# Indices of a gather staged by pairs, consumers two boundaries behind TensorE, and gates on two bank pairs in turn

## The chip, the cores and the metric

The kernel runs on one core of one Trainium2 chip. The metric is the device time of one execution in microseconds; three executions of the kernel before took 2054.03, 2059.32 and 2064.04 us, median 2059.32.

## The reference

One step of a one-layer decoder for a prompt of 512 tokens and a sample group of 64 tokens (8 sequences of 8). Both run through the same layer, in float32:

```python
[q | k | v | u] = x @ w_in + b_in
att  = three dilated causal windows with ALiBi, merged by their softmax denominators
y    = S5 state-space groups over u; z = gelu(y); ssm = z * sigmoid(z @ w_glu + b_glu)
h    = LN1(ALPHA * x + concat(rms(att), rms(ssm)) @ w_out + b_out)
out  = LN2(ALPHA * h + PEER(h) + sigmoid(h @ w_ple_gate) * (p @ w_ple))

def PEER(x):                       # in blocks of 128 tokens, 8 heads
    q = x @ w_pq                   # two halves of 128 per head
    s1, s2 = q1 @ sub_keys1.T, q2 @ sub_keys2.T
    # top 16 of each, top 16 of their 256 sums -> 16 experts e of 16384, weights g = softmax
    a = gelu(x . peer_u[e]); return sum over 8 x 16 experts of g * a * peer_v[e]
```

The sample group attends to a cache of 2048 positions per sequence. Each token reads 128 rows of `peer_u` and 128 of `peer_v`, 1024 floats each; the kernel keeps both in one table, so a gathered row is 8 KB.

## The kernel before

Tokens are five blocks: four of 128 prompt tokens (b = 0 to 3) and one of 64 sample tokens (b = 4). A front part projects the input, runs the state-space scan and takes block 0 to its first experts. Then comes one long loop over the experts.

**The loop.** A step gathers one expert row for each of 128 partitions (1 MB) into one of eight ring slots (`RING`, `HALF` = 4, `PAIR` = 2). There are 576 steps, 288 pairs. A partition holds one (token, head part) item: four groups of 32 tokens share a block. For each pair, in program order on each engine:
- POOL (L803 to L812) waits until the indices are staged and the slot is free, and issues the gather.
- DVE (L2013) waits for the landing and multiplies the `u` half with `hrep`, h spread to the gather's layout, and sums: `dotted`.
- ACT (L1544 to L1560) waits for `dotted`; at the second pair of a half it copies the half's next four indices as integers (`copy_stage`, L1502, `staged`); then gelu, times the weight, and a 128x32 selection matrix for each slot (L1559, `diagonal`).
- PE (L1262) multiplies that matrix with the slot's `v` half, adds into two PSUM banks, and frees the slot (`slot_free`).

**The background.** All other work is put between pairs: attention of blocks 1 to 3 (`scores` L868 on PE, `bias` L1703 on DVE, `exps` L1349 on ACT, `turn_probs` L883 on PE, `copy_pt` L1358 on ACT, `values` L893 on PE, `norm_out` L1366 on ACT), output projections (`project` L1042, `residual_half` L1975), the questions to the key tables (`ask` L1208, `ask_out` L1484, `match` L1223, `match_out` L1492), the selection on DVE (`tops`, `cross`, `resolve`, L1887 to L1943) and `lay` (L1515) on ACT, decode attention on the cache (`s_scores` L1050, `s_values` L1096), and the gates (`gate` L1180, `gate_out` L1471 on ACT and L2024 on DVE, `finish`). `order_of_work` (L199) is a table written by hand: `at[p]` lists what stands at boundary p, ahead of pair p. Every engine walks through the same list in order and does its part of each entry; between engines there are only semaphores. So when ACT and PE both have a part at boundary p, ACT's part waits for PE's, and ACT's next pair behind it waits too.

**Block edges.** Blocks change at pairs 64, 128, 192 and 256. There h of the next block is spread: eight matmuls (`spread`, L1240) and eight copies into `hrep` (L1533), two of each at boundaries -3, -2, -1 and 0 of the edge. Around the edge the two slots of a pair belong to one group of 32 tokens (`token_groups`, L68).

**SP** (from L589) issues all other loads in a fixed order behind semaphores: weights as their places come free, the cache's keys and values for the eight sequences (`keys`, `values`, L672 to L681), then the sample block's and the gates' weights.

Of the kernel before, what the change touches and what calls it, by code (L numbers as in the profile page):

```python
# [17 lines left out]
P = 128  # L18
# [103 lines left out]
def order_of_front():  # L122
# [7 lines left out]
    for n in range(steps + 1):  # L130
# [38 lines left out]
        if n == 14:  # L169
# [5 lines left out]
              ("ask_out", 0, 1), ("ask_out", 0, 2), ("match", 0, 1)] + [("spread", 0, n) for n in range(8)]  # L175
# [9 lines left out]
ATT_AT = 2  # L185
GLU_AT = 7
RMS_AT = 33
PROJECT_AT = 33
LOOK_AT = 48
DECODE_AT = 128  # L190
DECODE_PAIRS = 8
SAMPLE_AT = DECODE_AT + DECODE_PAIRS * (NB - 1) + 10
SAMPLE_PICK_AT = SAMPLE_AT + 18
GATE_AT = SAMPLE_PICK_AT + 28
# [4 lines left out]
def order_of_work():  # L199
# [9 lines left out]
    at[GLU_AT + 2 * (QB - 1)].append(("take_sums",))  # L209
    for k in range((QB - 1) * NH // 2):  # L210
        two = [NH + 2 * k, NH + 2 * k + 1]
        qb = two[0] // NH
        t = ATT_AT + 2 * k
        for p, what in ((0, "scores"), (1, "bias"), (2, "exps"), (2, "turn_probs"), (3, "copy_pt"), (3, "invert"),
                        (4, "values"), (5, "norm_out")):
            at[t + p] += [(what, i) for i in two]
        if two[1] % NH == NH - 1:
            at[t + 6] += [("squares", qb), ("turn_att", qb)]
            at[t + 7].append(("att_out", qb))
            at[t + 8].append(("keep_squares", qb))  # L220

    def pick(n, *when):
# [3 lines left out]
        for x in range(2):  # L226
            at[when[4 + x]].append(("cross", b, c, x))
            at[when[6 + x]].append(("resolve", b, c, x))
            at[when[7] + 1 + x].append(("lay", b, c, x))

    def look(t, n):
# [3 lines left out]
        at[t + 2] += [("ask_out", b, c)]  # L235
        at[t + 3] += [("match", b, c)]
        at[t + 4] += [("match_out", b, c)]

    pick(1, *range(8))
    pick(2, *range(10, 26, 2))  # L240
    pick(3, *range(26, 42, 2))

    at[RMS_AT] += [("rms", 1), ("rms_root", 1)]
    at[RMS_AT + 1].append(("rms_inverse", 1))
    for b in range(1, QB):
        for half in range(2):
            t = PROJECT_AT + 4 * (b - 1) + 2 * half
            at[t].append(("project", b, half, 0))
            at[t + 1].append(("project", b, half, 1))
            at[t + 2].append(("residual_half", b, half))  # L250
        at[t + 3].append(("root", b))
        at[t + 4].append(("normal", b, 0))
        at[t + 5].append(("normal", b, 1))
    at[LOOK_AT - 7].append(("turn", 1))
    at[LOOK_AT - 6].append(("turn_out", 1))
    look(LOOK_AT - 5, 4)
    look(LOOK_AT, 5)
    for n in range(4, 4 * QB):
        t = LOOK_AT + 8 * (n - 4)
        pick(n, *range(t, t + 8))  # L260
        if n + 2 < 4 * QB:
            look(t + 2, n + 2)
        if n + 3 < 4 * QB and picks[n + 3][1] == 0:
            at[t + 7].append(("turn", picks[n + 3][0]))
            at[t + 8].append(("turn_out", picks[n + 3][0]))
# [12 lines left out]
    at[t].append(("s_gelu",))  # L278
    at[t + 1].append(("s_glu",))
    at[t + 2].append(("s_gate",))  # L280
    at[t + 3].append(("s_product",))
    at[t + 4].append(("s_att",))
    at[t + 5].append(("s_sums",))
    at[t + 6] += [("s_project", 0), ("s_scale",)]
    at[t + 7] += [("s_project", 1), ("rms_root", 2)]
    at[t + 8].append(("s_residual",))
    at[t + 9].append(("root", QB))
    at[t + 10].append(("normal", QB, 0))
    at[t + 11].append(("normal", QB, 1))
    at[t + 12].append(("turn", QB))  # L290
    at[t + 13].append(("turn_out", QB))
    look(t + 14, 4 * QB)
    for c in range(4):
        t = SAMPLE_PICK_AT + 8 * c
        pick(4 * QB + c, *range(t, t + 8))
        if c < 3:
            look(t + 2, 4 * QB + c + 1)

    for k, b in enumerate(FINISHED):
        t = GATE_AT + GATE_PAIRS * k  # L300
        at[t].append(("gate_turn", b))
        at[t + 1].append(("gate_turn_out", b))
        at[t + 2].append(("gate", b, 0, 0))
# [1896 lines left out]
```

## Time and profile before

| what | value |
|---|---|
| median of three runs | 2059.32 us |
| the profiled execution's own time | 2070.46 us |
| its span | 2068.6 us |
| mean granted TensorE clock | 0.856 |
| busy: PE, DVE, ACT, POOL | 1567.7, 1342.2, 776.8, 762.9 us |
| bytes moved | 718.95 MB, mean 348 GB/s |
| first gather issued | 293.9 us |
| last dot product starts | 2052.2 us |

Engines are PE (TensorE matmuls), PEld (its weight loads), DVE (VectorE), ACT (ScalarE), POOL (GpSimd) and SP (its queue issues plain DMAs). Times in the rows are microseconds from the span's start unless marked ns. "L1262" is a line of the kernel before. The clock is the share of full speed that was granted. A DMA share of 1.01 is full.

### The profile page before, as it was taken

How to read it: one execution, taken by the hardware profiler on the slowest of the kernel's cores; microseconds unless marked ns; L12 is line 12 of the kernel's file. 1: busy time of each engine (PE TensorE's matmuls, PEld its weight loads, DVE VectorE, ACT ScalarE, POOL GpSimd, SP SyncE). 2: the span in 40 equal slices, each digit the busy share in tenths (PEclk: the TensorE clock that was granted, in tenths of full speed). 3: DMA queues.
4: the chain of work that ended last, by engine and by line, in shares of the span. 5: the costliest groups of instructions: out<-in, count | busy, mean ns of one | idle time of the engine just before them, and what ended most of it. 6: DMA issues, size and time to landing. Idle time of an engine off the chain costs nothing.

```text
span 2068.6 us, 23469 instructions
## 1 busy us (share of the span) xinstructions
PE 1567.7 (76%) x7166; PEld 724.3 (35%) x7166; DVE 1342.2 (65%) x3188; ACT 776.8 (38%) x2630; POOL 762.9 (37%) x797
## 2 busy tenths in 40 slices
PE   7998696775877887767787766666885567789884
PEld 5674473332334343334322222222222234222221
DVE  6975647665768778888868444444344777655554
ACT  2132134764344444444444433323322333434442
POOL 0942213333334344444433333333233333443442
PEclk9999698788999989888898788878887886888987
DMA  7013157889999899999999999999999999988996
GB/s 282 1 62 102 70 205 325 332 325 398 396 384 420 349 380 421 419 419 415 413 393 412 401 421 410 422 413 424 359 412 423 422 421 381 402 333 334 364 358 279
DMA packets 103326, 718.95 MB, mean 348 GB/s; under 512 B 11696, under 2 KB 16560, under 8 KB 23600
## 3 DMA queue, kind: packets, MB, share of 16 engines
q0 software_dynamic: 82944, 604.02, 72.2%
q1 hardware_dynamic: 20272, 113.58, 13.8%
q8 instruction: 56, 0.92, 0.2%
q14 instruction: 54, 0.44, 0.1%
HBM read 712.69 MB, written 4.87 MB: 347 GB/s over the span
## 4 chain that ended last, share of the span: by engine, by line
PE 47%; DMA 26%; DVE 14%; ACT 6%; issue 6%; POOL 2%; POOLq 0%; ACTq 0%; SPq 0%; DVEq 0%
DMA R<-d_uv,W 25%; PE bank L1262 17%; DVE R L2013 8%; PE bank L854 5%; PE bank L1208 4%; PE bank L1050 3%; PE bank L1180 3%; PE bank L847 2%; POOL R L809 2%; ACT W L1554 2%; PE bank L1240 2%; PE bank L925 1%; PE bank L1096 1%; ACT W L1559 1%; ACT L1551 1%
## 5 line engine op out<-in xcount | busy, mean ns | idle before, releaser
L1262 PE MATMUL bank<-R,W 128*32 128x512 f32 x2304 | 794.2, 743 | 451.0 <-ACT W L1559 450.3
L809 POOL DMA_INDIRECT R<-d_uv,W x576 | 659.3, 1145 | 1114.6 <-ACT W L1502 536.3
L2013 DVE CUSTOM_DVE_ANT_0 R<-R,W 128x1024 f32<-128x1024 f32 x576 | 692.6, 1222 | 388.6 <-DMA R<-d_uv,W 385.2
L1262 PEld LDWEIGHTS bank<-R,W 128*32 128x32 f32 x2304 | 214.3, 125 | 928.2 <-ACT W L1559 637.5
L1502 ACT CAST W<-W 128x4 uint32<-128x4 f32 (+1 forms) x146 | 28.0, 193 | 453.8 <-DVE W L2013 453.6
L1559 ACT ACTIVATE W<-W 128x32 f32<-128x32 f32 x576 | 153.6, 314 | 9.4
L1551 ACT ACTIVATE W<-W 128x2 f32<-128x2 f32 x288 | 57.9, 201 | 254.2 <-DVE W L2013 253.2
L1554 ACT ACTIVATE W<-W 128x1 f32<-128x1 f32 x576 | 138.2, 287 | 10.3
L1551 ACT ACT_TABLE_LOAD x58 | 74.4, 1283 | 99.1 <-DVE W L2013 98.6
L854 PE MATMUL bank<-E,W 128*128 128x288 f32 x384 | 102.1, 424 | 11.7 <-DMA E<-d_xT 9.6
L1208 PEld LDWEIGHTS bank<-E 128*128 128x128 f32 x768 | 96.3, 207 | 26.4 <-issue 26.4
L1208 PE MATMUL bank<-E 128*128 128x128 f32 (+1 forms) x768 | 100.5, 294 | 0.0
L854 PEld LDWEIGHTS bank<-E,W 128*128 128x128 f32 x384 | 74.6, 198 | 33.3 <-issue 11.8
L1050 PE MATMUL bank<-E,W 128*64 128x512 f32 (+1 forms) x192 | 73.9, 527 | 0.0
L1180 PE MATMUL bank<-E 128*128 128x512 f32 (+1 forms) x160 | 73.1, 599 | 0.0
L1515 ACT COPY W<-E 32x16 f32<-32x16 f32 (+2 forms) x288 | 60.8, 211 | 7.3 <-DVE E L1943 3.9
L2024 DVE TENSOR_TENSOR W<-E,bank 128x512 f32<-128x512 f32 (+1 forms) x10 | 6.9, 687 | 76.3 <-ACT E L1471 76.3
L1887 DVE MAX8 E<-W 128x8 f32<-128x128 f32 (+3 forms) x120 | 40.1, 334 | 23.3 <-ACT W L1492 21.9
L1533 ACT COPY W<-bank 128x512 f32<-128x512 f32 x36 | 21.1, 586 | 88.2 <-PE bank L1240 88.2
L925 PE MATMUL bank<-E,R 32*128 32x128 f32 x256 | 34.5, 338 | 19.5 <-DVE R L1737 17.8
L2013 DVE DVE_READ_ACCUMULATOR2_ANT W<- 128x1 f32 x576 | 47.1, 82 | 0.0
L1042 PE MATMUL bank<-E 128*128 128x512 f32 x96 | 44.9, 610 | 0.0
(318 smaller groups left out, 1814.7 us busy)
## 6 DMA issues: line engine op xcount, KB each, us to landing
E<-d_kc SPq DMA_DIRECT2D x8, 2560.0 KB, 21.1
E<-d_w_pq SPq DMA_DIRECT2D x6, 2048.0 KB, 12.6
E<-d_vc SPq DMA_DIRECT2D x8, 1536.0 KB, 26.7
R<-d_uv,W POOLq DMA_INDIRECT x576, 10.9
E<-d_w_out SPq DMA_DIRECT2D x4, 2048.0 KB, 12.0
E<-d_vc SPq DMA_DIRECT2D x8, 1024.0 KB, 30.8
W<-d_w_in SPq DMA_DIRECT2D x3, 2048.0 KB, 18.1
R<-d_w_pq SPq DMA_DIRECT2D x3, 2048.0 KB, 13.0
```

The lines of the kernel that those rows point to most:

```text
L809: pool.indirect_dma_start(ring[r], None, A["uv"], bass.IndirectOffsetOnAxis(ap=stage[:, half, s:s + 1], axis=0),).then_inc(landed[r], 16)
L854: last = mm(bank[:, piece_bank(n), 0:WIDE], w[:, k, c * P:c * P + P], xT[:, k, x * WIDE:x * WIDE + WIDE], start=(k == 0), stop=(k == DC - 1))
L925: last = mm(bank[:, 6 + x, j * P:j * P + P], Bt[r, q, x, :], uT[r, q, b * P:b * P + P], start=True, stop=True)
L1050: last = mm(bankf[0:ST, n0:n1], qblk[:, b, c, :], kcS[:, c, n0:n1], start=(c == 0), stop=(c == CT - 1))
L1180: last = mm(bank[0:m, to, :], hT[:, k, 0:m], w[:, k, :], start=(k == 0), stop=(k == DC - 1), skip_group_check=True)
L1208: last = mm(bank[:, (2, 0)[c % 2], j * P:j * P + m], w[:, k, j * P:j * P + P], hT[:, k, 0:m], start=(k == 0), stop=(k == DC - 1))
L1262: last = mm(acc[TG * js[s]:TG * js[s] + TG, half * 512:half * 512 + 512], wsel[:, r, :], ring[r][:, D + half * 512:D + half * 512 + 512], ...
L1515: last = nc.scalar.copy(egall[TG * s:TG * s + TG, :, c0:c0 + (g1 - g0 - 1) * groups + 1:groups], eg[TG * j:TG * j + TG, :, 8 * s + g0 - 8 ...
L1551: f(gel[:, x, two], dots[:, x, two], ACT.Gelu_apprx_tanh).then_inc(gelued, 1)
L1554: last = f(wts[:, x, s:s + 1], gel[:, x, s:s + 1], ACT.Copy, scale=egall[:, 1, column(i, x * HALF + s, 1)])
L1559: f(wsel[:, x * HALF + s, :], fold[:, 0:TG], ACT.Copy, scale=wts[:, x, s:s + 1]).then_inc(diagonal, 1)
L2013: last = nc.vector.tensor_tensor_reduce(ring[r][:, 0:D], ring[r][:, 0:D], hrep[:, js[s], :], 1.0, 0.0, ALU.mult, ALU.add, dots[:, x, s:s + 1])
```

## The change

**Indices by pairs.** Both staging copies, ahead of the loop and in it, now cover two indices, one copy for every pair; POOL waits for `staged` ahead of each pair of gathers instead of each half.

**The table.** Consumers of PE's background work are put further behind it. `spread` is split: the copies are an entry of their own, `spread_out`, one boundary after the matmuls. In attention the bias stands two boundaries behind the scores (it was one), exponentials and transposes at +3, the copies at +5, the values at +6 and `norm_out` at +8 (they were at +2, +3, +4 and +5); steps still begin every two boundaries. `ask_out` stands two boundaries behind the last `ask`, `match_out` two behind `match`, the residual two behind the projection. The projections reach over 17 boundaries instead of 12. Block 1's first selection is squeezed into boundaries 54 to 59. Decode takes seven boundaries a sequence instead of eight and begins at 134 instead of 128.

**Gates.** `gate_out` on ACT becomes `gate_sigmoid`, two boundaries behind the matmuls, and the product on DVE one further; the two halves of a gate and the transposes of the next one use banks (0, 1) and (2, 3) in turn (`gate_banks`) instead of fixed ones. `finish`'s root is an entry of its own.

```diff
+    order += [(what, 0, n) for n in range(8) for what in ("spread", "spread_out")]
-        for p, what in ((0, "scores"), (1, "bias"), (2, "exps"), (2, "turn_probs"), (3, "copy_pt"), (3, "invert"),
-                        (4, "values"), (5, "norm_out")):
+        for p, what in ((0, "scores"), (2, "bias"), (3, "exps"), (3, "turn_probs"), (5, "copy_pt"), (5, "invert"),
+                        (6, "values"), (8, "norm_out")):
...
     for b in range(1, BLOCKS):
         for n in range(8 if b < QB else 4):
             at[BLOCK_PAIRS * b - 3 + n // 2].append(("spread", b, n))
+            at[BLOCK_PAIRS * b - 2 + n // 2].append(("spread_out", b, n))
...
+        def gate_banks(b, half):
+            return 2 * ((FINISHED.index(b) + half + 1) % 2)
...
             with pool.Fori(0, STEPS // RING) as i:
                 for half in range(2):
-                    pool.wait_ge(staged, 2 * i + half + 1)
                     for s in range(HALF):
                         r = half * HALF + s
+                        if s % PAIR == 0:
+                            pool.wait_ge(staged, i * (RING // PAIR) + (2 * half + s // PAIR + 1))
...
-                    pe.wait_ge(gate_used, 2 * n)
-                turn_h(b, BLOCKS + n)
+                    pe.wait_ge(gate_used, 2 * n - 1)
+                turn_h(b, BLOCKS + n, gate_banks(b, 1))
...
-                to = 2 - 2 * half
+                to = gate_banks(b, half)
                 if part == 0:
-                    pe.wait_ge(ht_ready, BLOCKS + FINISHED.index(b) + 1)
+                    pe.wait_ge(ht_ready, BLOCKS + n + 1)
+                    if half == 0 and n >= 1:
+                        pe.wait_ge(gate_used, 2 * n)
...
-            def copy_stage(half, at):
-                return nc.scalar.copy(stage[:, half, :], egall[:, 0, at])
+            def copy_stage(half, x, at):
+                return nc.scalar.copy(stage[:, half, PAIR * x:PAIR * x + PAIR], egall[:, 0, at])
...
-                h1 = p1 // 2
-                if (h1 + 1) * HALF < QB * EXP:
-                    act.wait_ge(laid, (h1 + 1) * HALF // (2 * PK) + 1)
+                last = (p1 + 2 * HALF // PAIR) * PAIR - 1
+                if last < QB * EXP:
+                    act.wait_ge(laid, last // (2 * PK) + 1)
...
                     act.wait_ge(dotted, n)
-                    if g == 1:
-                        copy_stage(x, column(i, RING + x * HALF, HALF)).then_inc(staged, 1)
+                    copy_stage(x, g, column(i, RING + x * HALF + g * PAIR, PAIR)).then_inc(staged, 1)
...
             def invert(i):
                 dve.wait_ge(p_ready, i + 1)
+                if i >= 4:
+                    dve.wait_ge(o_normed, i - 3)
...
-                tt(gp[0:m, n % 2, half * 512:half * 512 + 512], sgm[0:m], bank[0:m, 3 - 2 * half, :],
+                tt(gp[0:m, n % 2, half * 512:half * 512 + 512], sgm[0:m], bank[0:m, gate_banks(b, half) + 1, :],
```

POOL's loop, the first half of the ring, before:

```order
L807 ISA [waits staged]
L809 DMA R<-d_uv,W 128x2048 [waits slot_free]
L807 REGISTER_ALU
L809 DMA R<-d_uv,W 128x2048 [waits slot_free]
L807 REGISTER_ALU
L809 DMA R<-d_uv,W 128x2048 [waits slot_free]
L807 REGISTER_ALU
L809 DMA R<-d_uv,W 128x2048 [waits slot_free]
L803 REGISTER_ALU
L807 REGISTER_ALU [waits staged]
```

and after:

```order
L830 ISA [waits staged]
L832 DMA R<-d_uv,W 128x2048 [waits slot_free]
L830 REGISTER_ALU
L832 DMA R<-d_uv,W 128x2048 [waits slot_free]
L828 REGISTER_ALU
L830 REGISTER_ALU [waits staged]
L832 DMA R<-d_uv,W 128x2048 [waits slot_free]
L830 REGISTER_ALU
L832 DMA R<-d_uv,W 128x2048 [waits slot_free]
```

The wait for `staged` stood ahead of four gathers and now stands ahead of two.

ACT at the edge to block 1 before, from the weights of the fourth pair ahead of the edge on (L1533 are the copies of the spread, L1502 stages the indices, L1551 to L1559 are one pair):

```order
L1559 ACTIVATE W<-W 128x32 [waits weighed]
L1559 ACTIVATE W<-W 128x32
L1533 COPY W<-bank 128x512 [waits spread_full] x2
L1502 CAST W<-W 128x4 [waits dotted,laid]
L1551 ACTIVATE W<-W 128x2
L1554 ACTIVATE W<-W 128x1 [waits gelued]
L1554 ACTIVATE W<-W 128x1
L1559 ACTIVATE W<-W 128x32 [waits weighed]
L1559 ACTIVATE W<-W 128x32
```

and after, where the copies are L1562, the staging L1531 and a pair L1578 to L1586:

```order
L1562 COPY W<-bank 128x512 [waits spread_full] x2
L1531 CAST W<-W 128x2 [waits dotted,laid]
L1578 ACTIVATE W<-W 128x2
L1581 ACTIVATE W<-W 128x1 [waits gelued]
L1581 ACTIVATE W<-W 128x1
L1586 ACTIVATE W<-W 128x32 [waits weighed]
L1586 ACTIVATE W<-W 128x32
L1562 COPY W<-bank 128x512 [waits spread_full] x2
L1531 CAST W<-W 128x2 [waits dotted,laid]
```

The rows look alike; what moved is that the same two copies now stand behind one pair more of ACT's than of PE's matmuls, and each pair has its own cast.

PE in the attention steps before, one step with two pairs of experts (L893 values, L883 transposes, L868 scores, L1262 experts):

```order
L893 MATMUL bank<-E 128x64 [waits o_normed,pt_ready]
L893 MATMUL bank<-E 128x64
L893 MATMUL bank<-E 128x64 [waits o_normed,pt_ready]
L893 MATMUL bank<-E 128x64
L883 MATMUL bank<-ident,E 128x128 [waits pt_ready,p_ready]
L883 MATMUL bank<-ident,E 128x128 x2
L883 MATMUL bank<-ident,E 128x128 [waits pt_ready,p_ready]
L883 MATMUL bank<-ident,E 128x128 x2
L868 MATMUL bank<-E 128x384 [waits sc_biased] x2
L1262 MATMUL bank<-R,W 32x512 [waits diagonal]
L1262 MATMUL bank<-R,W 32x512
L1262 MATMUL bank<-R,W 32x512 [waits diagonal]
```

and after (L906 transposes, L1288 experts, L916 values, L891 scores):

```order
L906 MATMUL bank<-ident,E 128x128 [waits pt_ready,p_ready]
L906 MATMUL bank<-ident,E 128x128 x2
L906 MATMUL bank<-ident,E 128x128 [waits pt_ready,p_ready]
L906 MATMUL bank<-ident,E 128x128 x2
L1288 MATMUL bank<-R,W 32x512 [waits diagonal]
L1288 MATMUL bank<-R,W 32x512
L1288 MATMUL bank<-R,W 32x512 [waits diagonal]
L1288 MATMUL bank<-R,W 32x512
L916 MATMUL bank<-E 128x64 [waits o_normed,pt_ready]
L916 MATMUL bank<-E 128x64
L916 MATMUL bank<-E 128x64 [waits o_normed,pt_ready]
L916 MATMUL bank<-E 128x64
```

Values, transposes and scores stood together; now the transposes stand at one boundary and the values with the scores at the next, with a pair of experts between.

## Rows read from the trace of the kernel before

**Rows 1.** Busy PE, PEld, DVE, ACT, POOL by stretch, us; clock, DMA share, GB/s.
```profile
320.00:2052.00 1732.00, 1282.01 (x5324) 531.46 (x5324) 1117.78 (x2687) 692.57 (x2399) 652.68 (x570) 0.85 0.97 393
345.00:500.00 155.00, 110.81 (x488) 54.84 (x488) 107.29 (x305) 100.09 (x304) 54.20 (x52) 0.82 0.90 343
500.00:600.00 100.00, 80.18 (x246) 31.09 (x247) 66.62 (x134) 35.37 (x130) 32.27 (x28) 0.89 0.96 389
700.00:750.00 50.00, 41.81 (x160) 17.60 (x161) 35.46 (x97) 23.66 (x78) 15.66 (x17) 0.93 0.80 309
750.00:1000.00 250.00, 182.05 (x837) 88.82 (x835) 218.40 (x596) 111.41 (x456) 109.99 (x98) 0.85 1.01 419
1000.00:1050.00 50.00, 39.10 (x148) 16.91 (x145) 36.46 (x97) 22.60 (x87) 20.09 (x17) 0.90 1.01 390
1050.00:1460.00 410.00, 283.91 (x1467) 103.59 (x1466) 209.40 (x465) 142.94 (x494) 140.40 (x126) 0.82 1.01 415
1460.00:1500.00 40.00, 34.38 (x157) 10.57 (x156) 14.80 (x24) 12.82 (x48) 10.03 (x9) 0.82 0.87 341
1700.00:1750.00 50.00, 39.08 (x144) 21.18 (x142) 37.49 (x101) 15.17 (x57) 18.27 (x16) 0.70 0.95 378
1800.00:1850.00 50.00, 42.88 (x126) 16.40 (x124) 30.25 (x51) 23.42 (x64) 25.46 (x18) 0.90 0.93 363
1850.00:1890.00 40.00, 35.20 (x78) 9.51 (x77) 17.80 (x29) 13.95 (x38) 12.04 (x11) 0.83 0.70 264
1890.00:2050.00 160.00, 127.71 (x362) 42.19 (x364) 83.77 (x139) 63.36 (x186) 70.94 (x54) 0.87 0.94 376
```

**Rows 2.** DMA queues of the page: packets, MB, share.
```profile
q0 software_dynamic: 82944, 604.02, 72.2%
```

**Rows 3.** Waits, whole span: us in total, times, longest.
```profile
POOL R L809 <- ACT W L1502: 536.3, 87, 27.3
POOL R L809 <- PE bank L1262: 456.8, 175, 8.4
...
ACT W L1533 <- PE bank L1240: 88.2, 36, 9.2
...
DVE W L2024 <- ACT E L1471: 76.3, 10, 14.2
```

**Rows 4.** Timeline, 419 to 425 us: start, length, idle before and releaser.
```profile
419.81 1.92 PE L1262 MATMUL bank<-R,W 128*32 128x512 f32 x8
419.91 0.56 DVE L1703 CUSTOM_DVE_ANT_0 E<-bank,E 128x384 f32<-128x384 f32 x1 [6.38 <-PE bank L868]
...
424.84 0.94 POOL L809 DMA_INDIRECT R<-d_uv,W  x1 [7.67 <-ACT W L1502]
```

**Rows 5.** The page's costliest groups: the cast that stages indices.
```profile
L1502 ACT CAST W<-W 128x4 uint32<-128x4 f32 (+1 forms) x146 | 28.0, 193 | 453.8 <-DVE W L2013 453.6
```

**Rows 6.** Timeline at two block edges.
```profile
710.57 0.59 ACT L1533 COPY W<-bank 128x512 f32<-128x512 f32 x1 [7.03 <-PE bank L1240]
...
712.99 0.94 POOL L809 DMA_INDIRECT R<-d_uv,W  x1 [12.69 <-ACT W L1502]
...
1861.05 6.50 PE L1262 MATMUL bank<-R,W 128*32 128x512 f32 x8 [1.74 <-ACT W L1559]
...
1863.15 0.69 DVE L2024 TENSOR_TENSOR W<-E,bank 128x512 f32<-128x512 f32 x1 [14.19 <-ACT E L1471]
```

**Rows 7.** Waits, 350 to 500 us.
```profile
DVE E L1703 <- PE bank L868: 25.6, 9, 6.4
```

**Rows 8.** DMA issues of the page: count, KB each, us to landing.
```profile
E<-d_kc SPq DMA_DIRECT2D x8, 2560.0 KB, 21.1
...
E<-d_vc SPq DMA_DIRECT2D x8, 1024.0 KB, 30.8
```

**Rows 9.** Busy time of L1358 alone by stretch.
```profile
345.00:500.00 155.00, 9.89 (x22) 0.82 0.90 343
```

**Rows 10.** Busy time of L1366 alone by stretch.
```profile
345.00:500.00 155.00, 6.11 (x24) 0.82 0.90 343
```

More of the change, by code:

```diff
@@ L184 @@
 BLOCK_PAIRS = EXP // PAIR
-ATT_AT = 2
+ATT_AT = 1
 GLU_AT = 7
[L187 to L194, printed above, removed]
+PROJECT_AT = 35
+LOOK_AT = 54
+DECODE_AT = 134
+DECODE_PAIRS = 7
+SAMPLE_AT = DECODE_AT + DECODE_PAIRS * (NB - 1) + 13
+SAMPLE_PICK_AT = SAMPLE_AT + 20
+GATE_AT = SAMPLE_PICK_AT + 24
 GATE_PAIRS = 8
@@ L234, in look, with project, norm @@
         at[t + 1] += [("ask", b, c, 1)]
[L235 to L256, printed above, removed]
+        at[t + 3] += [("ask_out", b, c)]
+        at[t + 4] += [("match", b, c)]
+        at[t + 6] += [("match_out", b, c)]
+    pick(1, *range(10))
+    pick(2, *range(10, 26, 2), 25, 26)
+    pick(3, *range(26, 42, 2), 41, 42)
+    t = PROJECT_AT
+    at[t + 1].append(("rms", 1))
+    at[t + 2].append(("rms_root", 1))
+    at[t + 3].append(("rms_inverse", 1))
+    def project(b, half, t, u):
+        at[t].append(("project", b, half, 0))
+        at[t + 1].append(("project", b, half, 1))
+        at[u].append(("residual_half", b, half))
+    def norm(b, t):
+        at[t].append(("root", b))
+        at[t + 1].append(("normal", b, 0))
+        at[t + 2].append(("normal", b, 1))
+    project(1, 0, t, t + 3)
+    project(1, 1, t + 2, t + 5)
+    norm(1, t + 6)
+    project(2, 0, t + 4, t + 7)
+    project(2, 1, t + 6, t + 9)
+    at[t + 9].append(("turn", 1))
+    norm(2, t + 11)
+    at[t + 11].append(("turn_out", 1))
+    project(3, 0, t + 10, t + 13)
+    look(t + 12, 4)
+    project(3, 1, t + 14, t + 17)
+    norm(3, t + 24)
     look(LOOK_AT, 5)
@@ L323, in order_of_work @@
             order += at[p]
-    return order + [("finish", QB, 0), ("finish", QB, 1)]
+    return order + [("finish", QB, 0), ("finish_root", QB), ("finish", QB, 1)]
 ORDER = order_of_work()
@@ L1156, in turn_h @@
                 for c in range(DC):
-                    last = nc.tensor.transpose(bank[:, c // 4, (c % 4) * P:(c % 4) * P + m],
+                    last = nc.tensor.transpose(bank[:, first + c // 4, (c % 4) * P:(c % 4) * P + m],
                                                hB[b][0:m, c * P:c * P + P], ident[0:m, 0:m])
@@ L1470, in gate_out @@
                     act.wait_ge(gate_used, n)
-                f(sgm[0:m], bank[0:m, 2 - 2 * half, :], ACT.Sigmoid).then_inc(gate_sig, 1)
+                f(sgm[0:m], bank[0:m, gate_banks(b, half), :], ACT.Sigmoid).then_inc(gate_sig, 1)
             def turn_out(b):
```

109 lines of the change are left out of this document (59 added, 50 removed).

## The prediction

> **What bounds the kernel now.** I read the view by stretches first, then the waits of the whole span, then the timeline at the places where the transfers run thin. From 320 to 2052 us the core moves 393 GB/s with its DMA engines 97% busy, while PE, DVE and ACT are busy for 1282, 1118 and 693 of 1732 us [rows 1]. The work there is 576 gathers of 604.02 MB in all, 1.05 MB each [rows 2]. In the undisturbed stretch from 750 to 1000 us the rate is 419 GB/s at a full DMA share [rows 1], so a gather takes 2.5 us and a pair of them 5.0. The loop is bound by transfers wherever the ring of eight slots is kept supplied, and it loses time only where it is not. At 419 GB/s the 1732 us would be 1732 x 393/419 = 1625: at most 107 us can come back, whatever the edit. The 320 us before and the 16 us after the last gathers are a chain that the change hardly touches.
>
> The Trainium skill, DMA: Bandwidth & Descriptors, section Specifications, gives about 358 GB/s as HBM's limit for one core. By that rule no edit of the order could gain anything here; the trace disagrees, with 419 over 250 us, and the trace decides. The fabric ceiling of 435 GB/s in the same table is kept by every row; by it the most that can come back would be 167 us instead of 107.
>
> Where the 107 us lie, each as length x (1 - rate/419) [rows 1]:
> - 345 to 500, attention of blocks 1 to 3 in the background: 28.1 us. 500 to 600, projections: 7.2.
> - The four block edges, at 700 to 750: 13.1; 1000 to 1050: 3.5; 1460 to 1500: 7.4; 1850 to 1890: 14.8. Together 38.8 us.
> - Gates, 1800 to 1850: 6.7; 1890 to 2050: 16.4. Together 23.1 us.
> - The sample block's projection and questions, 1700 to 1750: 4.9. Decode, 1050 to 1460: 3.9.
>
> Together 106.0 us.
>
> **Staging by pairs.** POOL waited 536.3 us for the staged indices (ACT L1502) and 456.8 us for PE to free a slot [rows 3]. Where transfers are full this costs nothing. Where they aren't it does: PE's eight matmuls of a pair end at 419.81 + 1.92 = 421.7 us, which frees two slots, but POOL, idle for 7.67 us, issues only at 424.84, released by the cast that stages four indices at once after the next pair's dot products [rows 4]. With pairs the first two indices would be there before the slots, and two of four gathers go out about 424.84 - 421.7 = 3 us earlier. That is 3 us more slack in every half ring, before the transfers run dry. In return ACT casts twice as often: 144 casts more at 193 ns [rows 5], 28 us. ACT is busy for 693 of 1732 us [rows 1], so it lies beside DVE's dots. It stands ahead of the gelu, so where the ring is thin it delays the weights: some 470 us of such stretches hold about 90 pairs, half of them with a new cast, 45 x 0.19 = 9 us at most, zero at best. I take 2, since the wait behind it ends in most rows on a landing or on DVE.
>
> **Block edges.** Today the copy of the spread h (ACT L1533) stands at the same boundary as its matmul (L1240). PE reaches that only after the previous pair's matmuls, and ACT can't weigh the next pair meanwhile: it waits 7.03 us until 710.57, POOL 12.69 until 712.99 [rows 6]. ACT's waits there sum to 88.2 us [rows 3]. After the change ACT weighs one pair between, so the copy finds a finished matmul. What comes instead: PE's third and later spreads wait for copies that stand behind that pair's weights on ACT, and the first pair of a block waits for all eight copies, two of them behind its own weights. PE needs those weights anyway; what is added is two copies of 0.59 us [rows 6]. What stays is that the edge pairs of matmuls take 6.5 us at 1861 [rows 6], more than the 5.0 of a pair's transfers. Bounds: nothing or all of 38.8. I take two thirds, 26 us: ACT's wait is what made POOL's gap, and what stays is the small excess of slow matmuls.
>
> **Attention.** In 350 to 500 us DVE stood for 25.6 us for scores (L1703 behind L868) [rows 7], 6.38 of them at 419.91 [rows 4]; they are queued on PE behind the values and behind the transposes, which wait for the exponentials. The change puts transposes and scores at different boundaries and the bias two boundaries behind. But DVE is busy for 107 of 155 us in 345 to 500, ACT for 100 and PE for 111 [rows 1]; in 155 - 28 = 127 us that would be 84, 79 and 87%, with every engine in order. So the bounds are 0 and 28, and I take half, 14 us. For the projections there is little engine wait to remove: 3 of 7.2.
>
> **Gates.** DVE waited 76.3 us for sigmoids in ten places [rows 3], 14.19 of them until 1863.15, where it held the dot products back [rows 6]. Afterwards the sigmoid stands two boundaries behind PE, the product one behind it, and the next turn goes to the other bank pair. PE is busy for 43 of 50 us from 1800 to 1850 and for 128 of 160 from 1890 to 2050 [rows 1], though, so it is the next to bind. Bounds 0 and 23; half, 11 us. The sample block: 2 of 4.9, since the granted clock was 0.70 there [rows 1] and its matmuls stay long.
>
> **Decode** is packed from eight to seven pairs. The bytes are the same, so this moves load, it removes none: 0. Keys are issued when the previous scores end; six boundaries become five, 5 x 5.0 = 25 us at least, against 21.1 us from issue to landing [rows 8]. The values, 30.8 us [rows 8], keep six boundaries: 30 us at the bare rate of gathers, more with the cache's own bytes among them. Bounds: 0 and 8 x 0.8 = 6 us of late values.
>
> **Sum.** 26 + 14 + 3 + 11 + 2 - 2 = 54 us. The profiled execution took 2070.46 us for a span of 2068.6; 2070.5 - 54 = 2016.5. The median of the runs shown is 2059.3, 0.5% below the profiled one, so the forecast is 2059.3 x 2016.5/2070.5 = 2005.6, say 2006 us. Its own range, with a third to three quarters of the 107 coming back, is 1982 to 2024.
>
> **Rivals.**
> - Nearly everything comes back: 80% of 107 is 86, 2059 - 85 = 1974. For it speaks that two separate slacks are added, 3 us in the staging and a boundary in the background; against it the engine loads at attention and the gates. 0.12.
> - Half as much comes back, 27 us: 2032. DVE and PE become the bound in the attention stretch, where they would have to be 84 and 87% busy in order, and PE at the gates; only the edges give what I take. 0.18.
> - No change, 2056: the slots aren't free earlier than the indices in most thin places (POOL's 456.8 us behind PE speak for it), and the edges lose the same time to slow matmuls. Against it are the gaps of rows 6, all of which end on ACT. 0.07.
> - Slower: where consumers stand further back, buffers come free later, and PE meets that at the very boundary at which it refills them. Per attention step of two pairs the next scores now wait for the previous biases, two of 0.56 us [rows 4], the next transposes for the previous copies, 9.89/22 x 2 = 0.9 us [rows 9], and the values for the previous normalisations, 6.11/24 x 2 = 0.5 us [rows 10]; each was a boundary earlier before. If PE stands through all of it, 12 steps cost 12 x 2.5 = 30 us and give none of their 14; at the edges PE then waits for ACT's copies as ACT waited for PE, and the 26 don't come. Left are 3 + 11 + 2 - 2 = 14 us of gain: 2059 + 30 - 14 = 2075. It decides from the point where PE gets to a boundary before ACT and DVE have left it, that is, where a pair's matmuls take less than its weights and background on ACT; today they take 1.92 us at 419.81 and 6.50 at 1861.05 [rows 4, 6], so at full clock it can, at half clock it can't. 0.11.
>
> **How the numbers follow.** The forecast has 0.52. A measurement of this kernel tells a change from about 0.5%, 10 us. Faster by more: 0.52 + 0.12 + 0.18 less 0.01 = 0.81; within 0.5%: 0.07 and that 0.01, 0.08; slower 0.11. The range reaches from 1974 to 2052: it holds the forecast, the half case and most of the large one, and leaves out most of the slower case.
>
> **What would show it.** Right: the rate from 700 to 750 us and at the later edges over 390 GB/s; ACT's waits for the spread under 30 us in all; DVE's waits for sigmoids under 25; DVE's wait for scores under 10; POOL's waits for ACT much shorter and those for PE longer; the stretch of 345 to 500 at 380 GB/s. Wrong: the rates in these stretches unchanged, with PE's waits for ACT and DVE at the attention steps grown by some 2 us each; or waits of PE's cache matmuls on their loads.

## The result and the profile after

| | before | changed |
|---|---|---|
| median of the comparison, us | 2061.68 (2054.03 to 2064.04) | 2026.99 (2023.65 to 2035.52, 4 runs) |
| ratio, 95% interval | | 0.9844 [0.9802, 0.9886] |
| median, measured a second time | 2063.74 | 2027.54 (2024.40 to 2031.51) |
| its ratio | | 0.9818 [0.9785, 0.9852] |
| profiled execution, us; span | 2070.46; 2068.6 | 2025.18; 2023.4 |

The change takes off 32 to 38 us; the forecast was 54, 2006 us against 2027. The time lies in the range (1974 to 2052) and just outside the forecast's own (1982 to 2024). "Faster by over 0.5%" came true. The profiled executions differ by 45 us, more than the medians: before's took 0.4% longer than the median of its comparison. The traces say where time went, the medians how much there was.

The view by stretches of the changed kernel, in the columns of [rows 1]:

```profile
320.00:2007.00 1687.00, 1248.89 (x5323) 516.99 (x5324) 1120.62 (x2687) 706.58 (x2538) 669.92 (x569) 0.87 0.99 403
345.00:500.00 155.00, 110.35 (x504) 51.99 (x502) 112.48 (x318) 104.43 (x329) 61.19 (x55) 0.85 0.96 388
500.00:600.00 100.00, 86.34 (x292) 34.06 (x289) 70.86 (x135) 40.41 (x152) 39.07 (x33) 0.90 1.00 406
650.00:720.00 70.00, 62.67 (x260) 30.26 (x260) 49.02 (x121) 32.25 (x118) 25.74 (x21) 0.93 0.81 302
750.00:1000.00 250.00, 180.76 (x911) 94.62 (x908) 222.16 (x607) 113.59 (x473) 114.70 (x100) 0.91 1.01 420
1000.00:1040.00 40.00, 34.36 (x124) 14.37 (x122) 33.90 (x90) 20.12 (x81) 13.89 (x12) 0.91 0.94 358
1450.00:1490.00 40.00, 36.03 (x182) 13.52 (x180) 15.88 (x34) 14.78 (x50) 11.98 (x12) 0.88 0.94 375
1830.00:1870.00 40.00, 40.00 (x101) 12.62 (x100) 22.34 (x36) 20.37 (x60) 18.16 (x14) 1.00 0.89 350
1870.00:2007.00 137.00, 107.85 (x332) 34.43 (x332) 78.44 (x126) 59.42 (x177) 53.60 (x48) 0.91 0.98 394
```

The whole loop now runs at 403 GB/s, from 393; the undisturbed stretch stays at 420. Attention went from 343 to 388 GB/s and the gates from 376 to 394. The first block edge stays thin, at 302 GB/s for 70 us, with PE busy for 62.7 of them, and none of the four edges reaches the 390 GB/s that the prediction asked for: 302, 358, 375 and 350 in the rows from 650, 1000, 1450 and 1830 us. The waits of the whole span (total, times, longest):

```profile
POOL R L832 <- PE bank L1288: 833.2, 263, 16.3
...
POOL R L832 <- ACT W L1531: 104.0, 16, 27.7
...
ACT W L1562 <- PE bank L1266: 62.7, 32, 7.4
...
DVE E L1732 <- PE bank L906: 10.7, 8, 3.4
DVE W L2055 <- ACT E L1497: 7.5, 2, 7.2
```

Against [rows 3]: DVE's wait for sigmoids fell from 76.3 to 7.5 us, and its wait for the scores (25.6 us in [rows 7]) is gone, while 10.7 us of waits for PE's transposes (L906) are new; ACT's wait for the spread fell only from 88.2 to 62.7, where under 30 was expected. POOL's wait for the casts fell by 432 us and its wait for PE grew by 376.

A rate over a fixed window mixes pairs that have moved. So the two timelines are also set against each other by the work itself: from the start of one pair's dot product to that of another, us. At 5.0 us for a pair's transfers the bound is in the last column.

```
pairs                                    before    after   change   at 5.0 us
0-32     attention in the background      204.9    184.8    -20.1       160
32-60    projections                      168.4    170.4     +2.0       140
60-76    first block edge                  94.2     97.7     +3.5        80
76-122                                    230.8    230.7     -0.2       230
122-140  second edge                      118.3    116.6     -1.7        90
140-186  decode of the sample group       304.1    310.4     +6.3       230
186-198  third edge                        90.5     82.4     -8.1        60
198-240                                   252.2    248.8     -3.4       210
240-252  gates                             71.3     63.1     -8.2        60
252-256  gates, fourth edge's spreads      27.0     19.1     -8.0        20
256-264  fourth edge, pairs behind it      54.3     48.4     -5.9        40
264-287                                   124.1    124.0     -0.1       115
start of the first pair                   309.5    308.4     -1.1
behind the start of the last pair          18.9     18.5     -0.4
```

The sum is the difference of the spans, 45.2, but for rounding. The sample block has half as many spreads as the others, and all four stand at boundaries 253 and 254 (`range(8 if b < QB else 4)` in the table), so the fourth edge begins in the row of 252 to 256, which it shares with the gates. Attention gave 20 us where 14 were forecast. The four edges, of which 26 us were expected, gave 20 with that row, but all of it at the third and fourth (22.0); the first two, worth 11 in the forecast, lost 1.8. The gates gave 8.2 up to pair 252 and a part of the 8.0 behind it, for 11. The decode's row grew by 6.3, where 0 was expected.

### The profile page after: what moved, and what is told of

Read it like the earlier page. It is cut to its first block, busy times and chain, and to the rows that moved or that the text cites. A ratio compares the mean times of both kernels' runs of the same rounds, so it can differ in the third digit from the quotient of the medians.

```text
span 2023.4 us, 23729 instructions
## 1 busy us (share of the span) xinstructions
PE 1535.5 (76%) x7166; PEld 709.8 (35%) x7166; DVE 1345.0 (66%) x3188; ACT 791.9 (39%) x2776; POOL 780.0 (39%) x797
## 4 chain that ended last, share of the span: by engine, by line
PE 43%; DMA 31%; DVE 13%; ACT 6%; issue 5%; POOL 1%; POOLq 0%; ACTq 0%; SPq 0%; DVEq 0%
DMA R<-d_uv,W 31%; PE bank L1288 15%; DVE R L2044 7%; PE bank L877 5%; PE bank L1206 3%; PE bank L1234 3%; PE bank L1073 3%; PE bank L870 2%; PE bank L1266 2%; PE bank L948 1%; ACT W L1581 1%; PE bank L1119 1%; POOL R L832 1%; PE bank L1202 1%; ACT L1578 1%
## 5 line engine op out<-in xcount | busy, mean ns | idle before, releaser
L1288 PE MATMUL bank<-R,W 128*32 128x512 f32 x2304 | 764.1, 720 | 433.9 <-ACT W L1586 433.3
L832 POOL DMA_INDIRECT R<-d_uv,W x576 | 677.4, 1176 | 1053.2 <-PE bank L1288 833.2
L1288 PEld LDWEIGHTS bank<-R,W 128*32 128x32 f32 x2304 | 208.8, 122 | 877.0 <-ACT W L1586 592.4
L1531 ACT CAST W<-W 128x2 uint32<-128x2 f32 x292 | 55.6, 191 | 870.1 <-DVE W L2044 869.9
L1586 ACT ACTIVATE W<-W 128x32 f32<-128x32 f32 x576 | 153.5, 313 | 9.4
L1234 PEld LDWEIGHTS bank<-E 128*128 128x128 f32 x768 | 87.6, 192 | 20.5 <-issue 20.5
L1234 PE MATMUL bank<-E 128*128 128x128 f32 (+1 forms) x768 | 91.5, 277 | 0.0
L877 PEld LDWEIGHTS bank<-E,W 128*128 128x128 f32 x384 | 74.6, 198 | 32.2 <-issue 10.7
L1578 ACT ACTIVATE W<-W 128x2 f32<-128x2 f32 x288 | 57.5, 200 | 0.9
L1918 DVE MAX8 E<-W 128x8 f32<-128x128 f32 (+3 forms) x120 | 40.0, 333 | 21.5 <-ACT W L1520 19.9
L1562 ACT COPY W<-bank 128x512 f32<-128x512 f32 x36 | 20.9, 587 | 62.7 <-PE bank L1266 62.7
L1921 DVE MAX8 E<-W 128x8 f32<-128x128 f32 (+3 forms) x120 | 40.5, 338 | 4.1
## 6 DMA issues: line engine op xcount, KB each, us to landing
E<-d_vc SPq DMA_DIRECT2D x8, 1536.0 KB, 25.5
```

Of the source, the lines that this page charges most:

```text
L832: pool.indirect_dma_start(ring[r], None, A["uv"], bass.IndirectOffsetOnAxis(ap=stage[:, half, s:s + 1], axis=0),).then_inc(landed[r], 16)
L877: last = mm(bank[:, piece_bank(n), 0:WIDE], w[:, k, c * P:c * P + P], xT[:, k, x * WIDE:x * WIDE + WIDE], start=(k == 0), stop=(k == DC - 1))
L1234: last = mm(bank[:, (2, 0)[c % 2], j * P:j * P + m], w[:, k, j * P:j * P + P], hT[:, k, 0:m], start=(k == 0), stop=(k == DC - 1))
L1288: last = mm(acc[TG * js[s]:TG * js[s] + TG, half * 512:half * 512 + 512], wsel[:, r, :], ring[r][:, D + half * 512:D + half * 512 + 512], ...
L1531: return nc.scalar.copy(stage[:, half, PAIR * x:PAIR * x + PAIR], egall[:, 0, at])
L1578: f(gel[:, x, two], dots[:, x, two], ACT.Gelu_apprx_tanh).then_inc(gelued, 1)
```

## The experiments

Each was measured in five rounds against the kernel before, whose median was 2063.7 us in the first group, 2066.2 in the second and 2065.1 in the third (the split alone, the step with scores apart and the last two kernels), which ran on another chip. The changed kernel itself ran in the first group only. Differences between experiments are differences of their ratios times 2062, and "the changed kernel" is then its second measurement (0.9818), taken in the same way; by the first (0.9844) every loss would be 5 us smaller and every gain 5 us larger. Each ratio is known to 5 to 7 us either way, so a difference of two of them under some 9 us isn't clear of the noise by the ratios alone; where a smaller one is used, the single times and the pair times of the traces are given with it.

### Is the result firm? The changed kernel again

> The changed kernel itself, as the yardstick for its neighbours on the same chip: ratio 0.984 to the kernel before, within 0.976 to 0.990.

2027.54 us, ratio 0.9818 [0.9785, 0.9852]. This is the level that the others of its kind are set against. Its ten executions in both measurements took 2023.65 to 2035.52 us. Between the traces of its two profiled executions the pair rows differ by up to 2.2 us.

### Staging by pairs alone, and the change without it

The first adds only the casts by pairs to the kernel before:

```diff
+                        if s % PAIR == 0:
+                            pool.wait_ge(staged, i * (RING // PAIR) + (2 * half + s // PAIR + 1))
...
-                    if g == 1:
-                        copy_stage(x, column(i, RING + x * HALF, HALF)).then_inc(staged, 1)
+                    copy_stage(x, g, column(i, RING + x * HALF + g * PAIR, PAIR)).then_inc(staged, 1)
```

> The kernel before with staging by pairs alone. Theory (staging gives 3 us of slack in each half ring, so it helps wherever ACT and DVE hold the ring, and POOL's wait moves from ACT to PE): 12 to 20 us faster, ratio 0.990 to 0.994, POOL's waits for ACT under 200 us. Rival (the gain is all in the order of the background; the slots are not free earlier than the indices): ratio 0.998 to 1.002, though POOL's waits change their name all the same.

2063.47 us, ratio 0.9995 [0.9973, 1.0017]: nothing that can be told, within 5 us either way. Its waits over the span, and from 350 to 500 us:

```profile
POOL R L810 <- PE bank L1263: 860.4, 246, 11.4
...
POOL R L810 <- ACT W L1504: 106.2, 15, 27.3
```

```profile
POOL R L810 <- PE bank L1263: 83.8, 22, 6.8
...
DVE E L1705 <- PE bank L869: 25.5, 7, 6.5
```

POOL's waits are much like those of the full change: 536 us behind the cast have become 106, and 457 behind PE 860. The time has not moved, and the stretch of 345 to 500 us runs at 345 GB/s, from 343. A wait can change its name almost completely and be worth nothing. Two reasons are possible, and no run tells them apart: the slots were the next release all along, or the gathers that went out earlier were not what DVE stood for. One pair row moved without moving the total: 122 to 140 took 124.8 us, from 118.3, so a few us in that row tell little. In the kernel before, DVE stood in 350 to 500 us for the scores for 25.6 us [rows 7] and for landings for less:

```profile
DVE R L2013 <- DMA R<-d_uv,W: 10.4, 5, 5.4
```

The second is the changed kernel with the casts by halves again:

> The changed kernel with the indices staged by halves again. If the two parts add up, 0.990 to 0.994 of staging is given back: ratio 0.990 to 0.995 to the kernel before. Rival (the background's order alone carries the gain): ratio 0.984, as the changed kernel. Third (the parts only work together, since with the background loosened the staging becomes the last wait): ratio 0.995 to 1.0.

2023.57 us, ratio 0.9808 [0.9775, 0.9841]: the same as with pairs. No gain of the staging shows in either company.

### The copy of the spread: back to its matmul's boundary, and the split alone

```diff
-            at[BLOCK_PAIRS * b - 2 + n // 2].append(("spread_out", b, n))
+            at[BLOCK_PAIRS * b - 3 + n // 2].append(("spread_out", b, n))
```

> The changed kernel with the copies of the spread back at the same boundary as its matmuls. Theory (PE bounds the edges, so it matters little who waits for whom): all four edges together 0 to 8 us slower than the changed kernel, ratio 0.982 to 0.986 to the kernel before. Rival (the added boundary is what gave the 14 us that the edges gained in the trace): 12 us or more slower, ratio 0.988 or above, with the last edge (pairs 256 to 264) back at 54 us from 48.

2057.53 us, ratio 0.9971 [0.9949, 0.9993]: 31 us of the gain are gone, and the rival of the expectation came true. In the trace the first edge's pairs take 105.5 us (from 97.7), the second's 128.8 (116.6), the third's 88.3 (82.4), pairs 252 to 256 25.5 (19.1) and 256 to 264 52.2 (48.4). ACT's wait for the spread is twice that of the changed kernel:

```profile
ACT W L1562 <- PE bank L1266: 123.3, 36, 14.1
```

The other way round, the kernel before with nothing but the split (the copy as an entry of its own, one boundary behind the matmul; the line that places it):

```diff
+            at[BLOCK_PAIRS * b - 2 + n // 2].append(("spread_out", b, n))
```

> The kernel before with the copies of the spread one boundary behind its matmuls, and nothing else. Theory (the split is worth some 30 us by itself; the changed kernel shows only half of it because its table puts questions on the first two edges): ratio 0.984 to 0.989, pairs 60 to 76 in 84 us or less, 122 to 134 in 74 or less. Rival (the split helps only together with the rest of the table): ratio 0.993 to 1.0.

2038.85 us, ratio 0.9888 [0.9859, 0.9917]: 23 us from this one edit. Here the first edge is cured as the prediction had it: ACT's wait for the spread falls from 88.2 [rows 3] to 10.5 us, and 650 to 720 us run at 409 GB/s.

```profile
ACT W L1535 <- PE bank L1242: 10.5, 18, 2.2
```

```profile
650.00:720.00 70.00, 60.42 (x235) 25.58 (x232) 61.72 (x169) 36.83 (x143) 31.05 (x27) 0.93 1.00 409
```

The same window holds earlier pairs here than in the changed kernel, whose pair 60 starts at 663.6 us and this one's at 680.2. Pairs 60 to 76 take 83.6 us at 402 GB/s, against 94.2 before and 97.7 in the changed kernel (359 and 337 GB/s). The expectation's other mark was missed: pairs 122 to 134, at the second edge, took 88.5 us where 74 or less was expected and the kernel before took 83.8 (88.8 with the staging alone), so no gain shows there. The third edge's row gave 6.0 us, pairs 252 to 256 gave 5.1 and 256 to 264 4.9. So the split works at the first edge, and something else in the change takes its gain back there.

### What takes it back: questions at the edge

PE's timeline in the changed kernel at the first edge (start, length, idle before and releaser; L1288 experts, L1234 questions, L1249 match, L1266 spread):

```profile
669.96 2.12 PE L1288 MATMUL bank<-R,W 128*32 128x512 f32 x8 [1.62 <-ACT W L1586]
...
686.70 3.62 PE L1288 MATMUL bank<-R,W 128*32 128x512 f32 x8
690.25 1.16 PE L1249 MATMUL bank<-E,W 128*128 128x128 f32 x8
691.24 3.74 PE L1234 MATMUL bank<-E 128*128 128x128 f32 x32
694.91 1.98 PE L1266 MATMUL bank<-E,W 32*128 32x512 f32 x4
696.82 3.62 PE L1288 MATMUL bank<-R,W 128*32 128x512 f32 x8
700.37 3.84 PE L1234 MATMUL bank<-E 128*128 128x128 f32 x32
704.14 1.98 PE L1266 MATMUL bank<-E,W 32*128 32x512 f32 x4
```

From there to 715 us PE has a single gap, of 0.68 us. Behind a pair of experts (3.6 us at an edge, against 2.1 at 669.96) stand questions (3.8) and two spreads (2.0), 9.3 us from 696.82 to 706.12 for a pair whose transfers take 5.0. ACT and POOL stand behind it:

```profile
705.29 0.59 ACT L1562 COPY W<-bank 128x512 f32<-128x512 f32 x1 [6.04 <-PE bank L1266]
```

```profile
711.42 1.45 POOL L832 DMA_INDIRECT R<-d_uv,W  x1 [9.23 <-PE bank L1288]
```

Over 679 to 716 us PE was busy for 36.32 of 37 us at the full clock, while the transfers ran at 270 GB/s:

```profile
679.00:716.00 37.00, 36.32 (x143) 16.02 (x143) 24.24 (x63) 14.50 (x48) 11.22 (x12) 1.00 0.75 270
```

The table of the background was shifted with the longer attention (`LOOK_AT`, where its look-ups start, is 54 instead of 48), and with that a block of questions for the next tokens, two batches of 3.8 us and a match, falls on boundaries 63 and 64, where the spreads are. One more block falls on 127 and 128, at the second edge. In the kernel before the questions stood at 58 and 59 and again from 66 on, and at 122 and 123. The first experiment moves the block of boundaries 63 to 69 four boundaries on:

```diff
-            look(t + (5 if starts or n == 4 else 1), n + 2)
+            look(t + (5 if starts or n in (4, 5) else 1), n + 2)
```

> The changed kernel with one question block (two asks of 3.8 us each and a match) moved from boundaries 63 to 68 to 67 to 73, off the first block edge. Theory (PE is the bound there, busy without a gap from 679 to 716 us): pairs 60 to 70 in 59 us instead of 66, the whole 5 to 8 us faster, ratio 0.978 to 0.980. Rival (DVE and ACT hold the ring there): the same 66 us and ratio 0.982.

2018.09 us, ratio 0.9777 [0.975, 0.9804], 8 us below the changed kernel, and all six executions (2011.78 to 2021.26) lie below its ten. Pairs 60 to 76 take 90.4 us instead of 97.7, and the edge runs at 349 GB/s:

```profile
650.00:720.00 70.00, 61.71 (x250) 29.17 (x251) 53.91 (x131) 34.55 (x124) 28.21 (x24) 0.93 0.90 349
```

That is half of the way to the 83.6 us of the split alone. The other suspect is the length of PE's expert pairs at the edges, where both slots of a pair go to the same 32 columns. Here they go to two groups, which changes what is summed there:

```diff
-                    js = token_groups(2 * i + x if isinstance(i, int) else p0 // 2)
+                    js = list(range(SG)) if m == P else [0, 1, 0, 1]
```

> The changed kernel, with PE's expert matmuls of the pairs at the block edges put into two groups of 32 columns as in the rest of a block, where the changed kernel has both slots of a pair in one group (this changes what is summed there; nothing else differs). Theory (PE bounds the edges: a pair takes 3.62 us at full clock there instead of 2.12): 4 edges x 4 to 8 pairs x 1.5 us, of which the starved ones count, 10 to 20 us faster than the changed kernel, ratio 0.975 to 0.979 to the kernel before, and over 370 GB/s from 650 to 720 us instead of 302. Rival (DVE and ACT hold the ring ahead of the first edge, with the squeezed selection, the normalisation and 5 us of lay): no change, 0.984, and the thin stretch from 655 to 720 stays.

2016.47 us, ratio 0.9773 [0.9735, 0.981]: 9 us below (2012.36 to 2025.26). Relieving PE at the edges in either way gives about the same; both say that PE's own work is a part of what binds there. ACT's wait for the spread goes to 44.5 us (from 62.7). It isn't all of it: the expectation asked for over 370 GB/s, and the row reaches 326, with PE busy for only 53.7 of the 70 us:

```profile
650.00:720.00 70.00, 53.71 (x266) 28.12 (x262) 52.82 (x127) 32.34 (x118) 28.69 (x26) 0.88 0.84 326
```

Block 1's squeezed selection on DVE (boundaries 54 to 59) and block 3's normalisation (59 to 61) stand ahead of this edge in the changed table too. No run moved them.

### Attention and gates at their old distances

The changed kernel with the old attention steps (one boundary between producer and consumer, scores with values and transposes):

> The changed kernel with the attention entries at their old distances. Theory (the attention's order gives what pairs 0 to 32 gained, 205 to 185 us): 16 to 22 us slower than the changed kernel, ratio 0.990 to 0.993. Rival (the projections and questions behind it, pairs 32 to 60, give it back): below 8 us, ratio under 0.986.

2038.57 us, ratio 0.987 [0.984, 0.99]; that is 11 us more, between the 16 to 22 of the expectation's theory and the 8 of its rival. In the trace pairs 0 to 32 take 203.8 us again, 19 more. The wait comes back to what it was (25.6 us in [rows 7]), and 345 to 500 us run at 345 GB/s again:

```profile
DVE E L1732 <- PE bank L891: 26.0, 9, 6.4
```

The changed kernel with the gates at their old distances, each half in its fixed bank pair and the transposes always in the second half's, as before:

> The changed kernel with the gates at their old distances and fixed banks. Theory (the gates gave what pairs 240 to 256 gained, 98 to 82 us): 12 to 18 us slower, ratio 0.988 to 0.991, DVE's waits for sigmoids back over 60 us. Rival (PE bounds the gates either way): below 5 us, ratio 0.984 or less.

2041.08 us, ratio 0.9891 [0.9863, 0.9919]: 15 us more. The wait for sigmoids is back at

```profile
DVE W L2055 <- ACT E L1497: 65.3, 10, 9.1
```

Pairs 240 to 252 take 73.4 us (from 63.1), 252 to 256 21.9 (19.1). Distance and banks were changed together and are not told apart.

### Is it the distance, or that scores stand apart?

An attention step with scores and values apart but one boundary shorter in three places (edit: `(1, "bias")`, `(4, "copy_pt")`, `(5, "values")`, `(6, "norm_out")` in place of 2, 5, 6 and 8, and what follows moved up by 2 or 3).

> The changed kernel with attention's consumers one boundary behind PE, as before the change, but transposes and scores at different boundaries, as after it. Theory (what freed the attention stretch is that the scores no longer stand behind the transposes and their exponentials on PE; DVE waited for scores): pairs 8 to 24 in 86 to 90 us, as in the changed kernel, not 105, ratio 0.980 to 0.984. Rival (the second boundary of distance is what counts): pairs 8 to 24 in 100 us or more, ratio 0.986 or above.

2100.29 us, ratio 1.0179 [1.0155, 1.0203]: slower than before by 37 us and than the changed kernel by 74. It does not answer the question, since it brought a third thing in: the bias of one step now stands at the boundary of the previous step's transposes, whose buffer it writes. Its waits from 350 to 500 us, and the row that is in them twice a step:

```profile
POOL R L832 <- PE bank L1288: 119.0, 18, 13.2
...
DVE E L1732 <- PE bank L906: 61.4, 8, 9.3
```

```profile
356.05 0.61 PE L906 MATMUL bank<-ident,E 128*128 128x128 f32 x4
356.59 0.42 DVE L1732 CUSTOM_DVE_ANT_0 E<-bank,E 128x256 f32<-128x256 f32 x1 [5.77 <-PE bank L906]
```

DVE, which holds the dot products, stands for 61.4 us until PE has read the old probabilities; pairs 0 to 24 take 214.5 us instead of 135.7, which is all of the loss. What it points to is the price of a reuse that falls on one boundary, a relative of the slower rival's mechanism, though there PE was to wait for ACT and DVE, and here DVE waits for PE. The three shorter distances were not tried one by one. In the changed kernel the same wait is there with 10.7 us.

### The second edge, and both remedies

The last two kernels also move the questions of the second edge from boundary 127 to 121 (`if n == 13: look(t - 5, n + 2)`), the last one with the casts by halves besides.

> The changed kernel with the question blocks of both edges moved away, the first to boundaries 67 to 73, the second from 127 to 121. Theory (PE bounds the edges, each block of questions costs there what it takes on PE, 8 to 9 us): ratio 0.972 to 0.975, pairs 128 to 134 in 41 to 44 us instead of 50. Rival (at the second edge the cache's loads and the move of h to the ring's banks hold it): no more than the first edge gave, 0.977 to 0.979.

2018.4 us, ratio 0.9771 [0.9748, 0.9795]: no more than with the first edge alone (0.9777), though pairs 122 to 140 take 112.3 us in its trace instead of 116.6. Pairs 128 to 134 fell from 49.9 to 34.3 us, below the 41 to 44 expected, but 122 to 128, nearer to where the questions now stand, rose from 29.7 to 45.7; so most of that time moved and did not go. What is left, 4.3 us, is no more than that row moves by itself. And the attention stretch, which this edit leaves alone, was slower in this trace: pairs 0 to 32 took 191.2 us, against 185.5 with the first edge alone, at a granted clock of 0.79 (0.84 there):

```profile
345.00:500.00 155.00, 117.33 (x496) 55.70 (x492) 109.44 (x313) 102.58 (x322) 58.75 (x53) 0.79 0.95 372
```

> The last kernel with the indices staged by halves again, 146 casts fewer on ACT. Theory (staging by pairs is worth nothing, since the thin stretches wait for engines, not for landings): within 0.2% of the last kernel. Rival (with the edges free the staging becomes the wait that ends last): 0.3 to 0.8% slower than the last kernel.

2009.77 us (2009.17 to 2018.21), ratio 0.9752 [0.9726, 0.9778]. This is the fastest version, 51 us below the kernel before and 14 below the changed one by the ratios; from the kernel just above it can't be told apart, as its expectation said. Its pairs 0 to 32 took 182.5 us. Its first edge:

```profile
650.00:720.00 70.00, 61.18 (x267) 28.74 (x263) 56.16 (x138) 35.55 (x127) 25.93 (x25) 0.95 0.89 355
```

## Why the prediction was right or wrong

**The bound**: right. The undisturbed stretch kept 420 GB/s, attention, projections and gates moved towards it, and 45 of the 107 us came back in the loop (1732 us are 1687).

**Staging by pairs**: the 2 us of cost stand within the error, but the argument was wrong. It counted 3 us more slack in every half ring; the kernel with this alone measures 0.9995. The prediction read the release of one gather (424.84 in [rows 4]) as time gained, while DVE stood for scores there. POOL's waits came out as announced, shorter for ACT and longer for PE, and so a sign on my list that holds without telling anything: it can't tell time that moved from time that was saved.

**Block edges**: the step that failed, at the first two edges. The forecast took two thirds of each edge's loss, 11 us for these two and 15 for the others; the traces show a loss of 1.8 (+3.5 and -1.7) and a gain of 22.0 (-8.1, -8.0 and -5.9, the -8.0 shared with the gates). The sum, 20 of 26, looks better than its parts. The mechanism of the split is shown by both runs on it: the split alone gives 23 us, and undoing it costs 31. What the prediction missed lies outside the edited lines. "What stays is the small excess of slow matmuls" took PE's load at the edge from the trace of before, while the shifted table brings two batches of questions to boundaries 63 and 64 and two more to 127 and 128, and none to the third and fourth edge. Moving one block gave 8 us back and took the first edge's pairs from 97.7 to 90.4 us; the split alone had them at 83.6, and the 7 us between are not explained. The questions were to be had blind: the order of PE's instructions at boundaries 61 to 65 shows them. The prediction looked at that order around the copies only. ACT's wait for the spread (62.7, expected under 30) and the rates at all four edges (302 to 375, expected over 390) both showed it.

**Attention**: 14 forecast, 20 in the traces, 11 when undone (19 in that trace's pairs 0 to 32). The wait of [rows 7] went from 25.6 us to nothing, and 345 to 500 us run at 388 GB/s (380 expected). The engine loads, for which I took only half, allowed this: DVE is busy for 112 of 155 us. Whether the distance or the separate boundaries did it isn't settled.

**Gates**: 11 forecast, 8 in pairs 240 to 252 of the traces and a part of the 8 behind them, 15 when undone. In pairs 252 to 256 undoing the gates brings 2.8 us back and undoing the split 6.5. The sigmoid's wait fell to 7.5 us (under 25 expected). PE as the next to bind does show, at 1830 to 1870 with 40.00 of 40.00 us busy at 350 GB/s; that is pairs 256 to 262, behind the fourth edge, a shorter place than feared.

**Projections and sample block**: 5 forecast, about 1.4 in the traces (+2.0 and -3.4), below what can be told. **Decode**: 0 to 6 us of late values were the bound, and its row grew by 6.3. The traces speak against late values: in neither does a wait of any engine end on a load of the cache. That the size agrees is chance. Decode now begins at boundary 134 instead of 128, so the row of 140 to 186 holds more of its work than before and that of 122 to 140 less, and it is packed into seven pairs a sequence instead of eight; no run varied either.

**The sum**: by the traces +2.0 for projections, -20.1 for attention, -20.2 for the edges (with 252 to 256), -8.2 for the gates, -3.4 for the sample block and +6.3 for decode, against my -3, -14, -26, -11, -2 and 0. Attention and the last two edges, both more than forecast, meet the first two edges and decode at 45 of 54 us; that they offset each other is luck. Before's profiled execution took 0.4% longer than its median; by medians 32 to 38 came. A slip besides: three quarters of 107 us give 1979 as the lower end of the forecast's own range, not 1982. The forecast scaled its time to the median, and should rather have asked whether the profiled execution's excess lies in the very gaps that the change closes.

**The rivals**: half as much (2032) was nearer in number than the forecast, for a reason it didn't have: it left the attention and gates out and kept the edges, while attention and gates gave and two of four edges did not. Of the slower one a relative was measured: where a write of DVE falls on the boundary of PE's last read the kernel lost 74 us, with DVE waiting for PE. In the changed kernel 10.7 us of such waits stand beside the 25.6 that went, and the waits that the rival feared don't show: none of PE for biases, copies or normalisations of the attention is in the trace (down to 0.2 us), and for the exponentials (L906 behind L1375) its matmuls waited 3.1 us and its weight loads 10.0.

**What stays open**: the undone parts (31, 11, 15, and nothing for the staging) sum to 57 us against 38 for the whole. If the parts add up, some 19 us of what they gain is lost in the shifted table, 8 us of it shown at the first edge; the rest isn't settled, and parts that act in the same pairs, as the split and the gates do in 252 to 256, needn't add up. The second edge's move is unproven either way: the 4 us in its trace are no more than that row moves by itself, and the same trace lost 6 us in the attention stretch.

## What to carry to other kernels

When one background list feeds several in-order engines, put a consumer one entry behind its producer, and look for the same at every reuse of a buffer: a copy beside its matmul cost 31 us here, and the kernel with a write beside the last read was 74 slower. Inserting entries shifts all that follow, so list what each engine has at its tightest places afterwards, even where no line of the diff names them; a good part of an edit's gain can be lost there. Choose the rows of a timeline by where the work stands, too: the fourth edge's spreads stood in pairs that first look like the gates'. And of a wait that an edit shortens ask what else ends at that time: 430 us of POOL's waits for the cast went, and the total did not change by anything that could be told.

## What the runs showed of the hardware

- One core moved 420 GB/s over 250 us and 403 over the 1687 us of the loop. The Trainium skill (DMA: Bandwidth & Descriptors, Specifications) gives about 358 GB/s as HBM's limit for a core. The Trainium skill, in the section Bandwidth of that page, says that a core gets about this when both cores of an HBM domain stream; here one core ran alone, so these rates do not refute it, and the prediction's "By that rule no edit of the order could gain anything here" took it for a case that this isn't. The table's 435 GB/s for the fabric is not exceeded by any row.
- The eight float32 matmuls of a pair, as the trace records them (128x32 by 128x512), took 3.62 us (686.70) when both slots went to one group of 32 columns and 2.12 us (669.96) when they went to different groups, both at a granted clock of 1.00. With the edge pairs in two groups the kernel was 9 us faster.
